# Two experts of 64 tokens in one gathered slot, multiplied in the two column halves of TensorE

## The chip, the cores and the metric

One Trainium2 chip, one core of it in use. The metric is device time in microseconds (us) of one launch, from the runs' own timer; the profile is one execution of the same program taken by the hardware profiler. TensorE appears as PE (matmuls) and PEld (weight loads), VectorE as DVE, ScalarE as ACT, GpSimd as POOL, SyncE as SP.

## What is computed

A two-layer backbone over 256 latent and 256 context tokens of width 1024. Each layer has a mixer (layer 0: a short gated convolution and a chunked gating MLP; layer 1: a conformer convolution and differential attention) and then a PEER channel mixer. All is float32. The mixer is left out here; the part that the change touches is this:

```python
def peer(h, wq, subkeys, u_tab, v_tab):
    t = h.reshape(-1, D_MODEL)
    q = (t @ wq).reshape(-1, PEER_HEADS, 2, PEER_QDIM // 2)
    s = jnp.einsum('thpd,hpkd->thpk', q, subkeys)
    sv, si = lax.top_k(s, PEER_TOPK)
    ...                      # 16 x 16 sums of both halves' scores, the best 16 of them
    idx = i1 * PEER_KEYS + i2
    g = jax.nn.softmax(cv, axis=-1)
    act = jax.nn.gelu(jnp.einsum('td,thkd->thk', tb, u_tab[ib]))
    return jnp.einsum('thk,thkd->td', gb * act, v_tab[ib])
```

Eight heads choose 16 of 16384 experts each, so every token reads 128 experts, and an expert is a row of `u_tab` and a row of `v_tab`, 1024 numbers each. The mixer is run three times: stage 0 (layer 0, latent tokens), stage 1 (layer 0, context tokens), stage 2 (layer 1, latent tokens).

## The kernel before, in words

Tokens lie on the 128 partitions; 256 tokens are two tiles. `u_tab` and `v_tab` are stored side by side, so an expert is one row of 8 KB in device memory. A **slot** is one expert for each of the 128 tokens of a tile: a gather of 128 rows, one per partition, into one of the eight places of the ring `uv`. There are 128 slots for a tile, 256 for a stage and 768 in all. For slot s:

- POOL (`gathers`, line 1050) waits until the place is free (`uv_used`) and issues the indirect transfer. The row numbers come from `idx`, a column per slot.
- DVE (`dot`, line 1593) waits for the landing and multiplies the u half with the tokens' rows `h2`, summing along the row: one number for each token.
- ACT (`weigh`, lines 1221, 1223, 1225) takes gelu of it, multiplies by the softmax weight `gw` and scales the identity with the result: `diag`, a 128 x 128 diagonal matrix.
- PE (`add_values`, line 983) multiplies `diag` with the v half, twice 512 columns, and sums in two banks of PSUM, `acc`, over the 128 slots of a tile. The last of the two matmuls raises `uv_used`.
- After the last slot of a tile DVE (`close`) multiplies `acc` by the gate and adds it to the token rows.

Everything else (projections, convolution, attention, queries, scores, the searches `find` that make `idx` and `gw`, conditioning) is cut into steps. `schedule` writes one list, `program`, in which slots, steps and values alternate: at slot s stands ("slot", s), then the takes that empty PSUM banks, then ("values", s - 2), as LAG is 2, then the steps whose place has come. Each engine walks this one list in its order (`walk`), doing its own part of every entry. So PE's order is values of one slot, some steps, values of the next, and PE does nothing at a "slot" entry, ACT and DVE nothing at "values".

`turn_back` (PE line 938, then ACT) makes the rows `h2` of a tile out of the transposed `hT`: eight transposes of 128 x 128 and two copies out of PSUM, once for each stage and tile, six in all. The first lies before slot 0, the first of stage 2 in the gap between slot 511 and slot 512; the others lie among slots. In front of slot 0 the places of the ring hold weights, and the first gathers wait for the products that read them (line 704 and line 768). `ada_pair` (line 704) multiplies conditioning weights in quarters of the array: for each k it issues quarters 0 and 1 out of one weight block and then quarters 2 and 3 out of the next block.

A search has six parts; the last (lines 1560 to 1576) writes the index of 16 experts (line 1564) and their weights (line 1569), one instruction each for a tile. Weights of the projections are loaded by SP through the same transfer engines.

## Time and profile before

| what | value |
|---|---|
| median of 3 runs | 2360.29 us (2359.01 to 2362.58) |
| span of the profiled execution | 2360.1 us |
| PE busy | 2079.7 us (88%), of which line 983 1447.1 us in 3072 records |
| DVE busy | 1609.6 us (68%), of which line 1593 935.1 us |
| ACT busy | 953.4 us (40%) |
| POOL busy | 1019.5 us (43%) |
| transfers | 939.43 MB, mean 398 GB/s |
| the chain that ended last | PE 36%, transfers 33%, DVE 13%, issue 7%, POOL 6%, ACT 5% |

Slots are gathered from 176 us on and from 1664 us on; before the one lies the first mixer, in between (1590 to 1664 us) the gap in which stage 1 ends and attention starts. A table of stretches shows, for each stretch, how long each engine was busy in it, the mean granted clock of PE and what was transferred. A line with "x12" stands for twelve records in a row.

### The profile page before, as it was taken

To read this page: it belongs to the slowest core of one execution; us is meant where nothing else is said; L and a number is where in the kernel's file an instruction comes from. 1 tells how busy PE (TensorE), PEld (TensorE's weight loads), DVE (VectorE), ACT (ScalarE), POOL (GpSimd) and SP (SyncE) were. 2 spreads that over 40 slices of the span, in tenths; PEclk is the share of its full clock that TensorE was granted. 3 is DMA by queue.
4 is the path that set the end of the run, shared out by engine and by line. 5 is a ranking of instruction groups with operands and counts; after the bars stand their busy time and mean duration, and the time that the engine had idled before them with its cause. 6 is when DMAs were issued, how large, how long until landed. Compare 5 with 4: busy or idle time off the path is not lost.

```text
span 2360.1 us, 24134 instructions
## 1 busy us (share of the span) xinstructions
PE 2079.7 (88%) x6896; PEld 1123.8 (48%) x6896; DVE 1609.6 (68%) x3952; ACT 953.4 (40%) x2791; POOL 1019.5 (43%) x868
## 2 busy tenths in 40 slices
PE   8998998899998988988898998798899988777787
PEld 7775554455564434544454544346455533222222
DVE  3855668967766568788866677855765887666454
ACT  2014434543334444444454333534543444444333
POOL 0004444344334444444444454530333555566774
PEclk9999999999999999999999999999999999999999
DMA  9979999999999999999999999996799999999997
GB/s 400 375 291 382 395 399 421 407 421 421 421 420 421 415 421 404 421 421 417 391 421 421 421 421 421 416 370 254 284 365 379 415 421 421 422 421 421 422 421 318
DMA packets 132595, 939.43 MB, mean 398 GB/s; under 512 B 14720, under 2 KB 17920, under 8 KB 18944
## 3 DMA queue, kind: packets, MB, share of 16 engines
q0 software_dynamic: 110592, 805.36, 82.8%
q1 hardware_dynamic: 21888, 132.68, 13.8%
q8 instruction: 55, 0.90, 0.2%
q14 instruction: 60, 0.49, 0.1%
HBM read 936.93 MB, written 1.05 MB: 397 GB/s over the span
## 4 chain that ended last, share of the span: by engine, by line
PE 36%; DMA 33%; DVE 13%; issue 7%; POOL 6%; ACT 5%; POOLq 0%; SPq 0%; DVEq 0%; ACTq 0%
DMA uv<-uv_dram,stage_idx 31%; PE psum L983 19%; PE psum L786 9%; DVE uv L1593 6%; POOL uv L1050 5%; PE psum L768 4%; PE psum L926 1%; DMA uv<-in_dram 1%; ACT diag L1225 1%; DMA uv<-ada_dram 1%; ACT wv L1223 1%; DVE h L1282 1%; PE psum L704 1%; PE psum L957 1%; ACT gel L1221 1%
## 5 line engine op out<-in xcount | busy, mean ns | idle before, releaser
L983 PE MATMUL psum<-uv,diag 128*128 128x512 f32 x3072 | 1447.1, 611 | 227.8 <-ACT diag L1225 217.6
L1050 POOL DMA_INDIRECT uv<-uv_dram,stage_idx x768 | 985.9, 1284 | 1052.3 <-PE psum L983 829.5
L1593 DVE CUSTOM_DVE_ANT_0 uv<-uv,h 128x1024 f32<-128x1024 f32 x768 | 935.1, 1226 | 554.6 <-DMA uv<-uv_dram,stage_idx 545.2
L983 PEld LDWEIGHTS psum<-uv,diag 128*128 128x128 f32 x3072 | 562.1, 192 | 1006.5 <-issue 505.3
L1221 ACT ACTIVATE gel<-dots 128x1 f32<-128x1 f32 x768 | 155.3, 202 | 1060.6 <-DVE dots L1593 1059.7
L1225 ACT ACTIVATE diag<-const,wv 128x128 f32<-128x128 f32 x768 | 308.3, 401 | 25.0
L786 PE MATMUL psum<-hT,wring 128*128 128x256 f32 (+1 forms) x1312 | 273.0, 361 | 0.7 <-ACT hT L1091 0.7
L786 PEld LDWEIGHTS psum<-hT,wring 128*128 128x128 f32 x1312 | 233.1, 190 | 60.2 <-issue 33.0
L1223 ACT ACTIVATE wv<-gel,gw 128x1 f32<-128x1 f32 x768 | 226.3, 295 | 25.0
L1038 POOL COPY stage_idx<-idx 128x8 uint32 (+1 forms) x96 | 33.4, 348 | 265.4 <-DVE idx L1564 264.7
L1073 ACT ACTIVATE work<-psum 128x256 f32<-128x256 f32 (+2 forms) x123 | 47.7, 389 | 128.5 <-PE psum L786 102.1
L768 PE MATMUL psum<-wring,hT 128*128 128x256 f32 x320 | 72.7, 382 | 0.7 <-ACT hT L1091 0.7
L768 PEld LDWEIGHTS psum<-wring,hT 128*128 128x128 f32 x320 | 61.6, 193 | 17.3 <-issue 8.8
L1221 ACT ACT_TABLE_LOAD x50 | 64.2, 1283 | 0.9
L1593 DVE DVE_READ_ACCUMULATOR2_ANT dots<- 128x1 f32 x768 | 62.8, 82 | 0.0
L786 PE MATMUL psum<-hT,uv 128*128 128x256 f32 (+1 forms) x224 | 52.4, 395 | 5.4 <-DVE sp_t L1364 2.8
L1532 DVE MAX8 work<-work 128x8 f32<-128x128 f32 x80 | 17.9, 279 | 50.8 <-ACT work L1073 50.7
L1401 DVE SCALAR_TENSOR_TENSOR work<-work,const 128x256 f32<-128x256 f32 x120 | 50.1, 478 | 0.0
L786 PEld LDWEIGHTS psum<-hT,uv 128*128 128x128 f32 x224 | 43.6, 208 | 13.3 <-issue 5.7
L1192 ACT ACT_TABLE_LOAD x32 | 41.1, 1283 | 0.6
L957 PEld LDWEIGHTS psum<-keys,work 128*128 128x128 f32 x192 | 26.6, 197 | 18.2 <-issue 11.6
L1282 DVE CUSTOM_DVE_ANT_0 h<-uv,h 128x1024 f32<-128x1024 f32 x28 | 33.2, 1221 | 3.0 <-issue 2.3
(224 smaller groups left out, 1289.8 us busy)
## 6 DMA issues: line engine op xcount, KB each, us to landing
uv<-ada_dram SPq DMA_DIRECT2D x30, 1024.0 KB, 15.8
wring<-in_dram SPq DMA_DIRECT2D x25, 1024.0 KB, 9.5
wring<-wq_dram SPq DMA_DIRECT2D x24, 1024.0 KB, 11.2
uv<-uv_dram,stage_idx POOLq DMA_INDIRECT x768, 14.2
uv<-in_dram SPq DMA_DIRECT2D x9, 1024.0 KB, 13.5
uv<-ada_t_dram SPq DMA_DIRECT2D x7, 1024.0 KB, 22.7
wring<-ada_dram SPq DMA_DIRECT2D x6, 1024.0 KB, 11.2
wring<-ada_t_dram SPq DMA_DIRECT2D x5, 1024.0 KB, 20.7
```

What stands on the lines that cost most here:

```text
L768: last = mm(bank[:, 0:BLK], src[:, k, :], w[:, k, :], start=(k == 0), stop=(k == KC - 1))
L786: last = mm(bank[:, 0:len(tiles) * P], w[:, k, i * P:(i + 1) * P], hT[:, k, tokens], start=(k == 0), stop=(k == KC - 1))
L957: last = mm(bank[:, o:o + P], qh[:, h % 2, q, t * P:(t + 1) * P], keys[:, h % 2, q * PK:(q + 1) * PK], start=True, stop=True)
L983: last = mm(acc[:, b, :], diag[:, s % RING, :], uv[:, s % RING, D + 512 * b:D + 512 * (b + 1)], start=(c == 0), stop=(c == NSEL - 1))
L1050: nc.gpsimd.indirect_dma_start(out=uv[:, s, :], out_offset=None, in_=tables[stage // 2], in_offset=bass.IndirectOffsetOnAxis(ap=stage_idx[ ...
L1073: mine.emptied(f(dst, src, func, **kw))
L1221: f(gel[:, r:r + 1], dots[:, r:r + 1], ACT.Gelu_apprx_tanh).then_inc(gelu_ready, 1)
L1223: f(wv[:, r:r + 1], gel[:, r:r + 1], ACT.Copy, scale=gw[:, (T // TT) % 2, T % TT, c:c + 1]).then_inc(wv_ready, 1)
L1225: f(diag[:, r, :], C("ident"), ACT.Copy, scale=wv[:, r:r + 1]).then_inc(diag_ready, 1)
L1282: v.tensor_tensor_reduce(out=row_tmp[:, j, :], in0=w, in1=c_rows[:, j, :], scale=1.0, scalar=0.0, op0=ALU.mult, op1=ALU.add, accum_out=ada ...
L1401: ops = [v.scalar_tensor_tensor(out=ccT[:, j, :], in0=cpT[:, j, k:k + TOK], scalar=w[:, j, k:k + 1], in1=ccT[:, j, :], op0=ALU.mult, op1=A ...
L1593: v.tensor_tensor_reduce(out=uv[:, r, 0:D], in0=uv[:, r, 0:D], in1=h2[:, row_of[stage], t, :], scale=1.0, scalar=0.0, op0=ALU.mult, op1=AL ...
```

## The change

A slot no longer holds one expert for each of 128 tokens but two experts for each of 64: partitions 0 to 63 hold the first expert, partitions 64 to 127 the second one, of the same 64 tokens. Slot 2m has tokens 0 to 63 of the tile, slot 2m + 1 tokens 64 to 127, both the experts 2m and 2m + 1. The number of slots, of rows and of bytes is the same. With it go:

- `diag` has 64 columns (two diagonals on top of one another, from `pair_ident`, which DVE makes once at the start), and the matmul writes 64 partitions of `acc`: the upper or the lower half, so the left or the right columns of the array. Contraction over 128 partitions sums both experts.
- the values of an even slot are put in the list right before those of the odd one, both at the place where the odd one's stood.
- `h2` has two forms for each tile, one for each half of tokens, with the 64 rows on both halves of the partitions; `turn_back` makes them by products with the identity, and ACT copies four banks.
- index and weight are written by four instructions instead of one, each for 64 partitions and every second column.
- the space that gathers' descriptors get in SBUF is set to 4096 bytes per partition.

```diff
+HALVES = 2
+HT = P // HALVES
+SCRATCH = 4096
@@ schedule
-            if v >= (0 if stage < 2 else first):
-                program.append(("values", v))
+            if v >= (0 if stage < 2 else first) and v % HALVES == HALVES - 1:
+                program += [("values", u) for u in range(v - HALVES + 1, v + 1)]
@@ build
-        h2 = sb("h2", [P, 2, TT, D])
+        h2 = sb("h2", [P, 2, TT, HALVES, D])
-        diag = sb("diag", [P, RING, P])
+        diag = sb("diag", [P, RING, HT])
+        pair_ident = sb("pair_ident", [P, HT])
+        ALL_HALVES = [(k, j) for k in range(HALVES) for j in range(HALVES)]
+        def rows_of(half):
+            return slice(half * HT, (half + 1) * HT)
@@ PE turn_back
-                for half in range(2):
-                    bank = to_act.open(pe)
-                    for i in range(4):
-                        last = turn(bank[:, i * P:(i + 1) * P], hT[:, half * 4 + i, t * P:(t + 1) * P], ident)
-                    to_act.fill(last)
+                for j in range(HALVES):
+                    half_tile = slice(t * P + j * HT, t * P + (j + 1) * HT)
+                    for half in range(2):
+                        bank = to_act.open(pe)
+                        for i in range(4):
+                            for k in range(HALVES):
+                                last = mm(bank[rows_of(k), i * P:(i + 1) * P], hT[:, half * 4 + i, half_tile], ident, start=True, stop=True)
+                        to_act.fill(last)
@@ PE add_values
+                j = c % HALVES
                 for b in range(2):
-                    last = mm(acc[:, b, :], diag[:, s % RING, :], uv[:, s % RING, D + 512 * b:D + 512 * (b + 1)],
-                              start=(c == 0), stop=(c == NSEL - 1))
+                    last = mm(acc[j * HT:(j + 1) * HT, b, :], diag[:, s % RING, :], uv[:, s % RING, D + 512 * b:D + 512 * (b + 1)],
+                              start=(c < HALVES), stop=(c >= NSEL - HALVES))
@@ ACT turn_back, weigh
-                for half in range(2):
-                    empty(h2[:, row_of[stage], t, half * 512:(half + 1) * 512], 512)
+                for j in range(HALVES):
+                    for half in range(2):
+                        empty(h2[:, row_of[stage], t, j, half * 512:(half + 1) * 512], 512)
-                f(diag[:, r, :], C("ident"), ACT.Copy, scale=wv[:, r:r + 1]).then_inc(diag_ready, 1)
+                f(diag[:, r, :], pair_ident[:, :], ACT.Copy, scale=wv[:, r:r + 1]).then_inc(diag_ready, 1)
+            act.wait_ge(pairs_set, 1)
@@ DVE find, last part
-                        v.scalar_tensor_tensor(out=idx[:, stage % 2, t, slots[i]], in0=w.side_no[:, a + i, :], scalar=float(PK),
-                                               in1=w.side_no[:, n_t + a + i, :], op0=ALU.mult, op1=ALU.add).then_inc(idx_ready[t], 1)
+                        for k, j in ALL_HALVES:
+                            done = v.scalar_tensor_tensor(out=pairs[rows_of(k), :, j], in0=first[rows_of(j), :, k], scalar=float(PK),
+                                                          in1=second[rows_of(j), :, k], op0=ALU.mult, op1=ALU.add)
+                        done.then_inc(idx_ready[t], 1)
...
+                        for half, j in ALL_HALVES:
+                            done = v.tensor_scalar(pairs[rows_of(half), :, j], terms[rows_of(j), :, half],
+                                                   w.e_stat[rows_of(j), 1, a + i:a + i + 1], None, ALU.mult)
@@ DVE dot, start
-                v.tensor_tensor_reduce(out=uv[:, r, 0:D], in0=uv[:, r, 0:D], in1=h2[:, row_of[stage], t, :], scale=1.0, scalar=0.0,
+                v.tensor_tensor_reduce(out=uv[:, r, 0:D], in0=uv[:, r, 0:D], in1=h2[:, row_of[stage], t, s % HALVES, :], scale=1.0, scalar=0.0,
+            v.tensor_tensor(pair_ident[:, :], C("ident")[:, 0:HT], C("ident")[:, HT:P], ALU.add).then_inc(pairs_set, 1)
@@ kernel
-    nc = bacc.Bacc("TRN2", target_bir_lowering=False, num_devices=1)
+    nc = bacc.Bacc("TRN2", target_bir_lowering=False, num_devices=1, dynamic_dma_scratch_size=SCRATCH)
```

## Rows read from the trace of the kernel before

**Rows 1.** The page's slices of 59 us: transfer rate.
```profile
GB/s 400 375 291 382 395 399 421 407 421 421 421 420 421 415 421 404 421 421 417 391 421 421 421 421 421 416 370 254 284 365 379 415 421 421 422 421 421 422 421 318
```
**Rows 2.** Stretches: length, busy us (instructions) PE, PEld, DVE, ACT, POOL; clock, share, GB/s.
```profile
200.00:330.00 130.00, 120.62 (x441) 73.89 (x440) 75.36 (x203) 53.51 (x161) 54.32 (x49) 0.99 0.99 397
...
470.00:920.00 450.00, 416.62 (x1257) 231.06 (x1256) 297.15 (x701) 177.88 (x540) 208.57 (x185) 1.00 1.01 420
...
1120.00:1180.00 60.00, 53.47 (x153) 28.50 (x153) 50.81 (x149) 27.89 (x81) 25.20 (x26) 0.97 0.97 392
...
1540.00:1590.00 50.00, 48.80 (x113) 20.96 (x112) 28.72 (x46) 19.49 (x62) 15.82 (x15) 1.00 0.92 361
...
1700.00:1760.00 60.00, 54.38 (x193) 30.40 (x192) 39.98 (x105) 28.32 (x76) 19.92 (x21) 1.00 0.92 361
...
1800.00:1840.00 40.00, 39.53 (x144) 25.04 (x143) 25.11 (x84) 17.82 (x53) 14.52 (x14) 1.00 0.92 353
1840.00:2330.00 490.00, 395.88 (x845) 149.35 (x843) 323.70 (x769) 196.60 (x612) 305.58 (x222) 0.98 1.01 421
```
**Rows 3.** The chain that ended last, in order of time: start, duration, what.
```profile
1575.89 10.42 DMA uv<-uv_dram,stage_idx
...
1797.00 3.47 PE psum L786 x16
...
1815.04 5.15 PE psum L983 x12
```
**Rows 4.** The same stretches, line 983 alone: length, PE busy, PEld busy, clock, share, GB/s.
```profile
200.00:330.00 130.00, 77.48 (x169) 30.91 (x168) 0.99 0.99 397
...
470.00:920.00 450.00, 300.53 (x657) 121.07 (x656) 1.00 1.01 420
...
1540.00:1590.00 50.00, 36.91 (x83) 15.71 (x84) 1.00 0.92 361
...
1700.00:1760.00 60.00, 33.73 (x74) 12.91 (x72) 1.00 0.92 361
...
1800.00:1840.00 40.00, 23.29 (x53) 10.07 (x54) 1.00 0.92 353
```
**Rows 5.** Waits from 200 to 330 us: us in total, times, longest.
```profile
POOL uv L1050 <- PE psum L983: 65.3, 25, 5.4
```
**Rows 6.** Timeline of PE from 1133 us: start, duration, records, [idle before].
```profile
1138.84 3.49 PE L983 MATMUL psum<-uv,diag 128*128 128x512 f32 x4 [1.88 <-ACT diag L1225]
```
**Rows 7.** Timeline of PE from 173.4 us: quarters of the array, line 704.
```profile
173.52 0.41 PE L704 MATMUL psum<-wring,silu_c 128*32 128x256 f32 x2
173.54 0.41 PE L704 MATMUL psum<-uv,silu_c 128*32 128x256 f32 x2
173.74 0.41 PE L704 MATMUL psum<-wring,silu_c 128*32 128x256 f32 x2
```
**Rows 8.** Line 1050, the gathers: time from issue to landing.
```profile
DMA to landing us min/median/max: 5.4/14.2/18.6
```
**Rows 9.** Timeline of all engines around the first turn_back (line 938) and first gather.
```profile
160.50 3.82 PE L786 MATMUL psum<-hT,wring 128*128 128x128 f32 x32
...
165.23 1.04 PE L938 MATMUL psum<-const,hT 128*128 128x128 f32 x8
...
165.87 1.08 ACT L1073 ACTIVATE h<-psum 128x512 f32<-128x512 f32 x2
...
176.04 1.09 POOL L1050 DMA_INDIRECT uv<-uv_dram,stage_idx  x1 [0.97 <-PE psum L704]
```
**Rows 10.** Groups of instructions by form: count, busy us, mean ns, idle before.
```profile
L1225 ACT ACTIVATE diag<-const,wv 128x128 f32<-128x128 f32 x768 | 308.3, 401 | 25.0
...
L1569 DVE TENSOR_SCALAR gw<-work 128x16 f32<-128x16 f32 x44 | 8.9, 239 | 1.0
...
L1564 DVE SCALAR_TENSOR_TENSOR idx<-work 128x16 uint32<-128x16 f32 x44 | 6.4, 172 | 1.0
```
**Rows 11.** The page's transfer queues: the gathers' queue.
```profile
q0 software_dynamic: 110592, 805.36, 82.8%
```

More of the change, by code:

```diff
@@ L506, in build @@
         row_of = (0, 1, 1)
-        c_rows = h2[:, 0, :, :]
-        row_tmp = h2[:, 1, :, :]
+        c_rows = h2[:, 0, 0, :, :]
+        row_tmp = h2[:, 1, 0, :, :]
         kept_sc = vx[:, :, :].rearrange("p a (b c) -> p (a b) c", c=2 * PK).rearrange("p h (q k) -> p h q k", q=2)
@@ L1563, in find @@
                     for i, t in enumerate(tiles):
-                        v.scalar_tensor_tensor(out=idx[:, stage % 2, t, slots[i]], in0=w.side_no[:, a + i, :], scalar=float(PK),
-                                               in1=w.side_no[:, n_t + a + i, :], op0=ALU.mult, op1=ALU.add).then_inc(idx_ready[t], 1)
+                        pairs = idx[:, stage % 2, t, slots[i]].rearrange("p (m j) -> p m j", j=HALVES)
+                        first, second = (w.side_no[:, q * n_t + a + i, :].rearrange("p (m k) -> p m k", k=HALVES) for q in range(2))
+                        for k, j in ALL_HALVES:
+                            done = v.scalar_tensor_tensor(out=pairs[rows_of(k), :, j], in0=first[rows_of(j), :, k], scalar=float(PK),
+                                                          in1=second[rows_of(j), :, k], op0=ALU.mult, op1=ALU.add)
+                        done.then_inc(idx_ready[t], 1)
                     dve.wait_ge(exp_ready, n["exp"])
@@ L1568, in find @@
                     link(v.reciprocal(w.e_stat[:, 1, a:b], w.e_stat[:, 0, a:b]))
-                    weights = [v.tensor_scalar(gw[:, stage % 2, t, slots[i]], w.e16[:, a + i, :], w.e_stat[:, 1, a + i:a + i + 1], None,
-                                               ALU.mult) for i, t in enumerate(tiles)]
-                    link(*weights[:-1])
+                    for i, t in enumerate(tiles):
+                        pairs = gw[:, stage % 2, t, slots[i]].rearrange("p (m j) -> p m j", j=HALVES)
+                        terms = w.e16[:, a + i, :].rearrange("p (m k) -> p m k", k=HALVES)
+                        for half, j in ALL_HALVES:
+                            done = v.tensor_scalar(pairs[rows_of(half), :, j], terms[rows_of(j), :, half],
+                                                   w.e_stat[rows_of(j), 1, a + i:a + i + 1], None, ALU.mult)
                     if kept(stage, h, tiles):
-                        link(weights[-1])
+                        link(done)
                     else:
-                        weights[-1].then_inc(sc_used, 1)
+                        done.then_inc(sc_used, 1)
                         dve.wait_ge(sc_used, k)
@@ L1601, in close @@
                 dve.wait_ge(*taken["gate", stage, 1])
-                tmp = h2[:, row_of[stage], t, :]
+                tmp = h2[:, row_of[stage], t, 0, :]
                 v.tensor_tensor(tmp, acc.rearrange("p a b -> p (a b)"), gate_peer[:, :], ALU.mult).then_inc(acc_free, 1)
```

8 lines of the change are left out of this document (4 added, 4 removed).

## The prediction

> **What bounds the kernel now.** I read the slices of the page first, then a table of chosen stretches, then the same table for line 983 alone, and only then single instructions. The slices show one number again and again: 421 GB/s [rows 1]. No slice is above 422, and in the table the stretches at 420 or 421 GB/s have a DMA share of 1.01 [rows 2]: the transfer engines are full there. A gathered slot moves 128 rows of 8 KB, 1.05 MB, which at 421 GB/s takes 2.49 us. 768 such slots are 1913 us of the 2360. In those stretches (470 to 920 us, 1840 to 2330 us, and most of what lies between 330 and 1540) nothing that is done on TensorE can make the kernel faster, however busy PE is.
>
> So what the change can be worth lies where the rate is below 421 while gathers run. For a stretch of length L at rate r the loss is L x (1 - r/421): 130 us at 397 lose 7.4 us; 60 at 392 (from 1120) lose 4.1; 50 at 361 (from 1540) lose 7.1; 60 at 361 (from 1700) lose 8.6; 40 at 353 (from 1800) lose 6.5 [rows 2]. From the stretch at 1540 I take off the end: the last gather of that stage is issued at 1575.89 and lands 10.42 us later [rows 3], so from 1586.3 to 1590 there is nothing to transfer; 3.4 us are left to win. Together 30.0 us, 25.9 without the stretch from 1120.
>
> Is PE what holds these stretches? In the four it is busy for 120.62 of 130, 48.80 of 50, 54.38 of 60 and 39.53 of 40 us [rows 2], and line 983, the values, is 77.48, 36.91, 33.73 and 23.29 us of that [rows 4]. GpSimd, which issues the gathers, waits there for line 983: 65.3 us in the first stretch [rows 5]. The stretch from 1120 is another case: there a slot's four records took 3.49 us where others take 1.72, after 1.88 us of idle [rows 6], and the granted clock of the stretch is 0.97 [rows 2]; that is the lower of the two levels for a few us.
>
> **The change, part by part.** *The values.* A slot has two float32 matmuls and each is two records, so four records of 512 columns; twelve in a row take 5.15 us [rows 3], 0.43 each, 1.72 per slot, 3.43 per pair. After it each matmul has the same 128 rows and 512 columns but writes 64 columns of the array, and the two slots of a pair write different halves. If the halves run side by side, a pair whose two diagonals are ready costs 1.72. Does hardware do that? The conditioning products (line 704) already use quarters. For each k the code issues quarters 0 and 1 from one weight block, then 2 and 3 from the other, each as two records, so four records of the first block stand in the program before four of the second. The trace shows two of wring and two of uv start within 0.04 us, and the next two of wring 0.22 us after the first [rows 7], just a record's time at 256 columns (3.47 us for 16, [rows 3]). So four quarters run at once, and the second record of a quarter that is still busy doesn't hold back the first of another. I take the full overlap: 0.86 us less per slot where PE is behind. Where PE is not behind, the odd slot's diagonal comes 2.5 us after the even one's, the halves run one after the other, and nothing changes.
>
> The Trainium skill speaks against this ("TensorE: Matmul & The Clock Gate", Part 3, The mechanism): matmuls start and end strictly in program order, none passes another. By that rule the second slot's first record could only overlap the first slot's fourth, and a pair would take seven records' time, 3.0 us. The alternation in the trace disagrees with it for quarters; for halves no row here decides.
>
> Half of line 983's time in the four stretches is 38.7, 18.5, 16.9 and 11.6 us, each more than the loss there (7.4, 3.4, 8.6, 6.5). PE would stop being last, and the transfers would be. Against it: going from full width to half width and back may cost something at each step that stands between pairs. Bounds: nothing, or one idle record of 0.43 us [rows 3]. In the first stretch the other work is 43.1 us, some 12 steps of 3.47, so 24 turns and at most 10 us of the 38.7 freed: no decision hangs on it, and I take nothing. As PE isn't full in two of the four (93% and 91%), part of the loss must be waits of other engines in turn. I take two thirds of 25.9: 17.3 us gained; ends 8 and 30.
>
> *The order.* Even slots' values move behind one more set of PE steps, up to 3.47 us later [rows 3], and the next gather into that slot with them; the odd ones lose the 1.72 of the even slot in front. The ring has eight slots, 19.9 us per turn at 2.49. From issue to landing it takes 14.2 us, and 5.4 at the least [rows 8]: 8.8 us of the flight are queueing, so a release later by 3.5 leaves the transfers full. I cost it at nothing; its price without that cover is among the rivals.
>
> *turn_back.* Eight records at 1.04 us [rows 9] become 32 matmuls, 64 records: no longer transposes but products with the identity, each chunk for both row halves. Records of 128 columns run at 3.82 us for 32 [rows 9], 0.119 each; side by side 32 of them in time, 3.8 us, so +2.8 per call; one after the other 7.6, +6.6. Four of the six calls lie inside streams of slots, beside transfers that are last. Two do not: before slot 0, where the first gather waits for line 704, which stands behind turn_back on PE [rows 9], and in the gap before slot 512, where PE's later steps (attention, queries) stand behind it and slots 512 on wait for PE. I count both: 5.6 us. ACT empties four banks in place of two, 1.08 us more [rows 9], beside PE's longer run.
>
> *The lists.* Index and weight of a head and tile become four instructions each: 3 x 0.172 + 3 x 0.239 = 1.2 us more DVE [rows 10], of which the three index ones, 0.5 us, are ahead of the gather. At slot 0 the wait for line 704 covers them; in the gap they are bare: 0.5 us. Elsewhere DVE delays a dot by 1.2 to 2.5 us per search, inside the 8.8 us of queueing.
>
> *Small ones.* The diagonal is 64 columns instead of 128, on ACT 401 ns now [rows 10]: at most half, 0.2 us, saved per slot, and no gain where transfers are last. One addition at the start, pair_ident, for which ACT waits: one DVE instruction, nothing to some 0.3 us, and I take nothing. The descriptor space given to gathers falls to 4096: 110592 packets for 768 gathers [rows 11] are 144 each, 9 per engine, 72 for all eight slots. The Trainium skill ("DMA: Bandwidth & Descriptors", Terms) gives a descriptor as 16 bytes, by which 4096 bytes would be 256 of them; no run here shows it. I take nothing.
>
> Sum: 2360.3 - 17.3 + 5.6 + 0.5 = 2349. The profiled execution's span is 2360.1 and the median 2360.29, so no shift is needed.
>
> **The rivals.** *Freed PE time doesn't become transfer time*: the stretches are a ring of waits (a search on DVE waits for scores on ACT, these for PE's queries, these for a bank), and only the lower end, 8 us, comes back: 2360.3 - 8 + 6.1 = 2358, no change that can be told. For it: PE's 7 to 9% idle there. Against: nearly 100% in the other two.
>
> *The halves don't overlap, in program order*: a pair takes 3.0 of 3.43 us, so 0.21 per slot, an eighth of line 983's time: 9.7 us of PE freed in the first stretch and 3 to 5 in the others; perhaps 8 us of transfer time, minus the 6.1: also 2358. So the change not doing what it says ends there too, not on the slow side.
>
> *The ring starves (slower)*: place: each search of a head, 24 in all, when a step of 3.47 us stands before an even slot's values and the longer search delays the odd dot. Dots are late by 1.2 to 2.5 us, the release by 3.47, and it decides once both together with the waits already there pass 8.8 us. If every search then costs the transfers 1 us, it is +24, with the gains of the forecast halved (8.6) and the costs 6.1: 2360 + 24 - 9 + 6 = 2381; at half of that 2369.
>
> *The clock*: PE is idle more, and with half the columns at work. At the lower level a four-record slot takes 3.49 us [rows 6]. From 470 to 920 the values would need 150 us as pairs and the rest 116 [rows 2, 4]; at the lower level all the time 532 of 450 us, far slower, but PE fits in as long as the lower level holds for under about 69% of the stretch (266 x 1.69 = 450). I see no row that speaks for so much.
>
> **How the numbers follow.** Forecast, gain beyond 0.2% (4.7 us, about what a measurement can tell): 0.53, own range 2333 (30 us back, one turn_back bare: 2360 - 30 + 3) to 2355. No change, by the first two rivals: 0.27 (0.18 and 0.09). Slower: 0.20, the ring 0.14, at 2369 to 2381, the clock 0.04 and the descriptor space 0.02, both far out. The range goes from 2333 to 2371: it leaves out a few hundredths below and half of the slow cases or a little more.
>
> **What would show it.** Right: in the changed trace records of line 983 of a pair start within hundredths of a us of each other in the stretches after slot 0 and after slot 512, those stretches read near 421 GB/s, and GpSimd's wait for line 983 there shrinks; the stretches at 421 stay as they are; the first gather comes about 3 us later. Wrong: pairs of 3 us or more where both diagonals are ready, new slices below 415 in the middle of a stage, a granted clock well under 0.97, or full overlap with the same rates as before.

## The result and the profile after

The kernel became slower, by a little: 2367.74 us median (2363.22 to 2372.6, 12 runs) beside 2362.14 (2358.87 to 2364.91, 12 runs) of the kernel before, a ratio of 1.0028 with a 95% interval of 1.0019 to 1.0036. The forecast was 2349, faster. The profiled execution spans 2368.4 us. In this section and the next a difference in microseconds is the ratio of a run less one, times 2362: the changed kernel stands at +6.6.

In the profile after, `add_values` is line 999 (983 before), the gathers 1066 (1050), the dots 1618 (1593), the diagonal 1242 (1225), `turn_back` 953 on PE and 1089 on ACT (938, 1073), index and weight 1585 and 1595 (1564, 1569), the projections 798 (786).

The page of after, busy time and slices; they answer to the table of before and [rows 1]:

```profile
PE 1935.7 (82%) x7232; PEld 909.9 (38%) x7232; DVE 1675.3 (71%) x4241; ACT 919.8 (39%) x2803; POOL 928.2 (39%) x868
...
GB/s 402 371 289 359 386 420 421 388 408 421 421 420 421 402 420 420 420 420 409 401 421 420 421 421 419 416 373 260 259 367 392 421 408 421 421 421 421 421 421 320
```

PE lost 144 us of work and the kernel still lost time. The slices say where: 359 and 386 from 177 us on were 382 and 395 before, 388 and 408 from 413 us on were 407 and 421, 259 from about 1655 us on was 284, and there are new ones at 402, 409 and 408 where 415 to 421 stood.

The stretches of after; columns as in [rows 2], and the row of before for 430 to 470 us, which the prediction did not read, in the second fence:

```profile
200.00:330.00 130.00, 108.73 (x495) 62.63 (x493) 77.22 (x205) 52.70 (x163) 53.13 (x50) 0.93 0.96 389
430.00:470.00 40.00, 33.05 (x116) 15.99 (x117) 38.12 (x119) 19.61 (x61) 16.36 (x15) 0.91 0.94 371
1540.00:1590.00 50.00, 45.35 (x123) 14.05 (x122) 29.82 (x48) 17.57 (x62) 20.29 (x19) 1.00 0.97 401
1700.00:1760.00 60.00, 50.43 (x244) 27.08 (x241) 41.29 (x106) 29.16 (x79) 23.25 (x22) 0.93 0.83 329
1800.00:1840.00 40.00, 37.56 (x161) 22.61 (x160) 28.34 (x81) 15.66 (x54) 15.94 (x16) 0.96 0.98 401
1840.00:2330.00 490.00, 362.91 (x847) 104.57 (x846) 344.14 (x859) 187.50 (x610) 239.01 (x220) 0.96 1.01 420
```

```profile
430.00:470.00 40.00, 36.43 (x111) 20.70 (x110) 35.32 (x106) 19.70 (x60) 15.39 (x14) 0.96 1.00 401
```

Two of the stretches that were to be won are won in part (353 became 401 from 1800 us, 361 became 401 from 1540), two are worse though PE is less busy in them (397 became 389, 361 became 329), and a new one is lost at 430 us, where DVE is busy for 38.12 of 40 us.

A stretch is fixed in time while the slots in it shift, so these rates are a first look. The gathers, counted in GpSimd's timelines, are surer. Beside before, the 32nd gather is issued 4.9 us later in the changed kernel, the 112th 8.8, the 512th 3.0, the 513th (the first after the gap) 6.6 and the last 8.4. So time is lost in the first 112 slots and after slot 511, and none on balance between them. This is one execution of each kernel.

PE, then GpSimd, of after from 263 us, in the first stretch (start, duration, records, [idle before]):

```profile
267.30 7.77 PE L798 MATMUL psum<-hT,wring 128*128 128x256 f32 x32
...
276.18 3.70 PE L999 MATMUL psum<-uv,diag 128*64 128x512 f32 x16
```

```profile
268.17 0.94 POOL L1066 DMA_INDIRECT uv<-uv_dram,stage_idx  x1 [8.46 <-PE psum L999]
...
278.93 1.06 POOL L1066 DMA_INDIRECT uv<-uv_dram,stage_idx  x1 [8.38 <-PE psum L999]
280.30 1.06 POOL L1066 DMA_INDIRECT uv<-uv_dram,stage_idx  x1 [0.31 <-issue]
```

The same engines in the trace of before; its two gathers belong to the slots of the last two above, the 33rd and 34th:

```profile
268.73 3.62 PE L786 MATMUL psum<-hT,wring 128*128 128x256 f32 x16
...
273.37 7.03 PE L983 MATMUL psum<-uv,diag 128*128 128x512 f32 x16
```

```profile
269.71 0.96 POOL L1050 DMA_INDIRECT uv<-uv_dram,stage_idx  x1 [4.04 <-PE psum L983]
276.06 1.19 POOL L1050 DMA_INDIRECT uv<-uv_dram,stage_idx  x1 [5.39 <-PE psum L983]
```

Sixteen records, four slots, take 3.70 us where sixteen full ones took 7.03: the halves do run side by side. But before them stand two projections in a row (x32, 7.77 us), and GpSimd waits 8.4 us, twice, for a place in the ring. Each time it then gets two places at once, so two slots waited 8.69 us here and 9.43 before: later and in bursts, but not longer. Its total wait for the values is no measure either. It grew over the kernel from 829.5 us to 913.9, while its own issues took 97 us less, and it is 944.5 in halves_alone below, which is faster than before.

### The profile page after: what moved, and what is told of

It reads as the page before. It is cut to its first block, busy times and chain, and to the rows that moved or that the text cites. A ratio compares the mean times of both kernels' runs of the same rounds, so it can differ in the third digit from the quotient of the medians.

```text
span 2368.4 us, 25105 instructions
## 1 busy us (share of the span) xinstructions
PE 1935.7 (82%) x7232; PEld 909.9 (38%) x7232; DVE 1675.3 (71%) x4241; ACT 919.8 (39%) x2803; POOL 928.2 (39%) x868
## 4 chain that ended last, share of the span: by engine, by line
DMA 41%; PE 26%; DVE 21%; issue 6%; ACT 5%; POOL 1%; POOLq 0%; SPq 0%; DVEq 0%; ACTq 0%
DMA uv<-uv_dram,stage_idx 39%; PE psum L999 11%; DVE uv L1618 9%; PE psum L798 7%; PE psum L780 3%; DVE gw L1595 1%; ACT diag L1242 1%; DMA uv<-in_dram 1%; PE psum L953 1%; POOL uv L1066 1%; ACT wv L1240 1%; DMA uv<-ada_dram 1%; DVE idx L1585 1%; DVE work L1579 1%; PE psum L716 1%
## 5 line engine op out<-in xcount | busy, mean ns | idle before, releaser
L999 PE MATMUL psum<-uv,diag 128*64 128x512 f32 x3072 | 1231.7, 640 | 350.6 <-ACT diag L1242 341.0
L1066 POOL DMA_INDIRECT uv<-uv_dram,stage_idx x768 | 888.8, 1157 | 1145.7 <-PE psum L999 913.9
L999 PEld LDWEIGHTS psum<-uv,diag 128*64 128x64 f32 x3072 | 333.6, 143 | 1147.7 <-ACT diag L1242 686.4
L798 PE MATMUL psum<-hT,wring 128*128 128x256 f32 (+1 forms) x1312 | 281.8, 369 | 0.7 <-ACT hT L1107 0.7
L1242 ACT ACTIVATE diag<-pair_ident,wv 128x64 f32<-128x64 f32 x768 | 267.1, 348 | 25.0
L1054 POOL COPY stage_idx<-idx 128x8 uint32 (+1 forms) x96 | 39.2, 409 | 270.6 <-DVE idx L1585 270.0
L972 PE MATMUL psum<-keys,work 128*128 128x128 f32 x192 | 33.6, 317 | 18.4 <-ACT work L1089 18.4
L1595 DVE TENSOR_SCALAR gw<-work 64x8 f32<-64x8 f32 x176 | 43.3, 246 | 3.2
L972 PEld LDWEIGHTS psum<-keys,work 128*128 128x128 f32 x192 | 27.0, 213 | 42.7 <-ACT work L1089 22.9
```

Of the source, the lines that this page charges most:

```text
L798: last = mm(bank[:, 0:len(tiles) * P], w[:, k, i * P:(i + 1) * P], hT[:, k, tokens], start=(k == 0), stop=(k == KC - 1))
L972: last = mm(bank[:, o:o + P], qh[:, h % 2, q, t * P:(t + 1) * P], keys[:, h % 2, q * PK:(q + 1) * PK], start=True, stop=True)
L999: last = mm(acc[j * HT:(j + 1) * HT, b, :], diag[:, s % RING, :], uv[:, s % RING, D + 512 * b:D + 512 * (b + 1)], start=(c < HALVES), stop ...
L1066: nc.gpsimd.indirect_dma_start(out=uv[:, s, :], out_offset=None, in_=tables[stage // 2], in_offset=bass.IndirectOffsetOnAxis(ap=stage_idx[ ...
L1242: f(diag[:, r, :], pair_ident[:, :], ACT.Copy, scale=wv[:, r:r + 1]).then_inc(diag_ready, 1)
L1595: done = v.tensor_scalar(pairs[rows_of(half), :, j], terms[rows_of(j), :, half], w.e_stat[rows_of(j), 1, a + i:a + i + 1], None, ALU.mult)
```

## The experiments

All numbers together, as ratio to the kernel before, run beside each on the same chip (95% interval), and difference:

| kernel | ratio | us |
|---|---|---|
| the changed kernel | 1.0028 (1.0019 to 1.0036) | +6.6 |
| before_pairs | 1.0020 (1.0009 to 1.0031) | +4.7 |
| before_narrow | 1.0036 (1.0024 to 1.0048) | +8.5 |
| before_space | 0.9997 (0.9986 to 1.0008) | -0.7 |
| one_half | 1.0125 (1.0109 to 1.0140) | +29.5 |
| own_place | 1.0083 (1.0069 to 1.0097) | +19.6 |
| pair_early | 1.0017 (1.0007 to 1.0026) | +4.0 |
| halves_alone | 0.9966 (0.9954 to 0.9979) | -8.0 |
| halves_early | 0.9959 (0.9946 to 0.9972) | -9.7 |
| old_lists | 0.9987 (0.9977 to 0.9996) | -3.1 |
| old_turn | 0.9986 (0.9973 to 0.9999) | -3.3 |
| turn_copies | 1.0010 (1.0001 to 1.0019) | +2.4 |
| lean | 1.0004 (0.9995 to 1.0012) | +0.9 |
| lean_both | 1.0002 (0.9990 to 1.0014) | +0.5 |
| lean_copies | 1.0002 (0.9992 to 1.0012) | +0.5 |

An interval is about 2 to 3 us to either side, so differences of two rows are good to 3 or 4 us. Several results lie outside the range that the theory they were made for had given, or between two ranges: one_half a little above its range, own_place and old_turn outside theirs, and before_pairs, before_narrow, halves_early, lean, lean_both, turn_copies and lean_copies between two.

**Overlap and order.** The first theory: the halves overlap, and the ring starves because values stand later in the list. Four kernels take order and overlap apart.

*one_half*, the changed kernel, all slots but the second of a tile in one half:

```diff
-                j = c % HALVES
+                j = 1 if c == 1 else 0
-                              start=(c < HALVES), stop=(c >= NSEL - HALVES))
+                              start=(c < HALVES), stop=(c == 1 or c == NSEL - 1))
```

> The changed kernel, but the values of all slots of a tile except the second go to the same half of the array's columns, so the two slots of a pair can't run side by side (the sums of the two token halves are mixed up by that). All waits, instructions and their order are those of the changed kernel. Theory A, with overlap worth the PE time that the records show: 6 to 20 us slower than the changed kernel, 2374 to 2388 us. If the overlap is worth nothing, since transfers or searches are last wherever PE is behind: 2366 to 2370 us. Rival C (clock): the granted clock rises, since PE is busy longer, towards 0.98.

Measured 2389.1 us. Overlap is worth 22.9 us beside the changed kernel. The run also shows that something costs much more than the forecast's 6.1 us: without overlap the change is 29.5 us slower than before.

*own_place*, the changed kernel with values at their own places:

```diff
-            if v >= (0 if stage < 2 else first) and v % HALVES == HALVES - 1:
-                program += [("values", u) for u in range(v - HALVES + 1, v + 1)]
+            if v >= (0 if stage < 2 else first):
+                program.append(("values", v))
```

> The changed kernel with one part undone: the values of every slot stand at their own place in the list again (slot s - 2), halves, lists, turn_back and descriptor space as changed. Theory A (the order costs the time: two sets of PE steps stand in a row before an even slot's values, its ring place and that of its neighbour come back late and together, and the transfers run dry): the new dips go, 2356 to 2362 us, and the stretches from 430 to 470 and 1700 to 1760 us are back near 401 and 361 GB/s. Rival B (the fixed additions cost it: turn_back, lists, descriptor space): stays at 2365 to 2369 us. Rival C (the lower clock costs it, because PE works with half the columns): stays at 2365 to 2369 us with a mean granted clock near 0.95.

2379.16 us. Slots then meet only where no step stands between them, and 13 us are lost beside the changed kernel; a part of that can be the changes of width priced below, of which single slots make more than pairs. So the pairs in the list are needed, and order is not the main cost.

*before_pairs*, the kernel before with pairs in the list and nothing else:

```diff
-            if v >= (0 if stage < 2 else first):
-                program.append(("values", v))
+            if v >= (0 if stage < 2 else first) and v % HALVES == HALVES - 1:
+                program += [("values", u) for u in range(v - HALVES + 1, v + 1)]
```

> The kernel before with one part of the change alone: the values of an even slot stand right before those of the odd one, at the odd one's place; 128 columns, old lists, old turn_back, old descriptor space. Nothing can overlap. Theory A: slower than before by 8 to 25 us (2370 to 2387), with dips where steps are dense (200 to 330 and 1700 to 1840 us). Rival B and C: no difference beyond 0.2%, 2358 to 2366 us.

2367.1 us, +4.7: moving values behind one more step has a price by itself, though its lower bound is only 2 us.

*pair_early*, the changed kernel with the pair where the even slot stood:

```diff
-            v = s - LAG
+            v = s - LAG + 1
```

> The changed kernel with the pair moved one place forward: both slots' values stand where the even slot's stood before the change (the odd one's now one slot behind its dot instead of two). The halves can still overlap. Theory A: both places come back earlier, 2346 to 2358 us, faster than before the change. Rival B: 2363 to 2369 us, as the additions stay. Rival C: 2363 to 2369 us. If PE's wait for the odd slot's diagonal now holds up the steps behind it (queries, so searches), it is slower than the changed kernel: 2370 to 2385 us.

2364.65 us, 2.6 better than the changed kernel, which is within the noise of such a difference, and still slower than before. The order may be a part of the loss; it isn't the loss.

**Width and additions.** own_place and one_half could be slow for two reasons: matmuls of half width, or the additional work in lists and turn_back.

*before_narrow*, the kernel before with half-width values that never overlap:

```diff
-        diag = sb("diag", [P, RING, P])
+        diag = sb("diag", [P, RING, 64])
...
-                    last = mm(acc[:, b, :], diag[:, s % RING, :], uv[:, s % RING, D + 512 * b:D + 512 * (b + 1)],
-                              start=(c == 0), stop=(c == NSEL - 1))
+                    last = mm(acc[64 * (c == 1):64 * (c == 1) + 64, b, :], diag[:, s % RING, :], uv[:, s % RING, D + 512 * b:D + 512 * (b + 1)],
+                              start=(c < 2), stop=(c == 1 or c == NSEL - 1))
...
-                f(diag[:, r, :], C("ident"), ACT.Copy, scale=wv[:, r:r + 1]).then_inc(diag_ready, 1)
+                f(diag[:, r, :], C("ident")[:, 0:64], ACT.Copy, scale=wv[:, r:r + 1]).then_inc(diag_ready, 1)
```

> The kernel before with only the width changed: the diagonal has 64 columns and every slot (but the second of a tile) writes the same 64 partitions of acc, each at its own place in the list; nothing overlaps, lists, turn_back and order are as before (half of the output is left out). Theory of the width: each change between full and half width costs about 0.2 us, some 0.4 for each round of one slot and one step, so where PE is last (200 to 330 us and 1660 to 1840 us, some 100 rounds) it loses 20 us or more: 2372 to 2390 beside 2361, nearly what own_place (2379) and one_half (2389) showed. Theory of the additions (lists and turn_back make these two slow, width is free as the prediction said): 2358 to 2363.

2369.06 us, +8.5: less than the theory of the width gave, but not nothing. The same piece of PE's work shows the price. First the kernel before, then before_narrow (start, duration, records):

```profile
1814.87 5.32 PE L983 MATMUL psum<-uv,diag 128*128 128x512 f32 x12
1820.03 3.62 PE L786 MATMUL psum<-hT,wring 128*128 128x256 f32 x16
1823.48 5.31 PE L983 MATMUL psum<-uv,diag 128*128 128x512 f32 x12
1828.63 1.05 PE L738 MATMUL psum<-gdiag,ones 128*128 128x128 f32 x8
1829.52 5.32 PE L983 MATMUL psum<-uv,diag 128*128 128x512 f32 x12
```

```profile
1820.03 5.36 PE L983 MATMUL psum<-uv,diag 128*64 128x512 f32 x12
1825.33 3.72 PE L786 MATMUL psum<-hT,wring 128*128 128x256 f32 x16
1828.98 5.36 PE L983 MATMUL psum<-uv,diag 128*64 128x512 f32 x12
1834.27 1.16 PE L738 MATMUL psum<-gdiag,ones 128*128 128x128 f32 x8
1835.36 5.36 PE L983 MATMUL psum<-uv,diag 128*64 128x512 f32 x12
```

From the first start to the last it is 14.65 us and 15.33 for the same work with four changes of width: 0.17 us for each change (0.14 from half to full, 0.20 from full to half). No half-width work stood next to full-width work in the trace of before, but the quarters of [rows 7] did. The record that follows their last step, which starts at 175.03 us:

```profile
175.39 0.38 PE L719 MATMUL psum<-const,ada_rows 128*128 128x4 f32 x2
```

Eight steps, 173.52 to 175.03, are 0.216 us from one to the next, but the full-width record starts 0.36 us after the last of them: 0.14 us more. So a price could be read before the change.

The mean granted clock of its trace is 0.990, beside 0.981 before, so half the columns at work do not by themselves lower the clock. The stretches of before_narrow, for [rows 2]; PE is as busy as before and the rates are lower:

```profile
200.00:330.00 130.00, 119.61 (x426) 60.65 (x425) 74.40 (x202) 51.19 (x160) 47.18 (x46) 1.00 0.97 384
...
1700.00:1760.00 60.00, 55.10 (x180) 24.50 (x179) 38.00 (x99) 27.02 (x74) 20.68 (x20) 1.00 0.88 336
1800.00:1840.00 40.00, 39.53 (x138) 20.96 (x137) 20.99 (x61) 12.66 (x44) 13.05 (x13) 1.00 0.86 323
```

*halves_alone*, halves, pairs and the diagonal of 64 columns put into the kernel before, whose lists and turn_back stay:

```diff
-            if v >= (0 if stage < 2 else first):
-                program.append(("values", v))
+            if v >= (0 if stage < 2 else first) and v % 2 == 1:
+                program += [("values", u) for u in (v - 1, v)]
...
-                    last = mm(acc[:, b, :], diag[:, s % RING, :], uv[:, s % RING, D + 512 * b:D + 512 * (b + 1)],
-                              start=(c == 0), stop=(c == NSEL - 1))
+                    last = mm(acc[64 * (c % 2):64 * (c % 2) + 64, b, :], diag[:, s % RING, :], uv[:, s % RING, D + 512 * b:D + 512 * (b + 1)],
+                              start=(c < 2), stop=(c >= NSEL - 2))
...
```

> The kernel before with values in two halves, 64-column diagonals and the order of pairs, but with the lists and turn_back of before (so it multiplies other rows than it should, its output isn't the reference's). It is the change without its additions on DVE and in turn_back. If lists and turn_back ate the gain: 2345 to 2356, the forecast. If order and width did: 2361 to 2367, within a few us of the changed kernel's 2368.

2354.68 us, faster than before by 8.0 us. This is the mechanism of the forecast at work. Its stretches, and PE from 286 us:

```profile
200.00:330.00 130.00, 109.43 (x454) 61.91 (x455) 80.93 (x216) 52.60 (x165) 53.55 (x52) 0.95 1.00 409
...
1700.00:1760.00 60.00, 51.40 (x221) 27.00 (x219) 39.50 (x99) 27.27 (x83) 20.16 (x22) 0.94 0.95 382
1800.00:1840.00 40.00, 34.51 (x131) 16.37 (x130) 31.16 (x89) 15.73 (x48) 22.99 (x20) 0.96 0.99 403
```

```profile
286.46 1.94 PE L983 MATMUL psum<-uv,diag 128*64 128x512 f32 x8
288.36 1.16 PE L957 MATMUL psum<-keys,work 128*128 128x128 f32 x8
```

A pair takes 1.90 us from its start to that of the next step, where two slots of full width take 3.43. Rates rise to 409, 382 and 403: PE isn't last there any more, but the transfers aren't full either. Counted as above, the same five gathers are issued 5.4, 5.0, 9.0, 5.0 and 10.4 us earlier than before. Beside the changed kernel that is 10.3, 13.8, 12.0, 11.6 and 18.8 us: what halves_alone leaves out costs time in the first 112 slots and after the gap, and next to nothing between them, where transfers are last.

*halves_early* is halves_alone with the one line of pair_early (`v = s - LAG + 1`):

> halves_alone with the pair at the even slot's place: the odd slot's values wait for a diagonal that is just being made, but no release of a place is late. halves_alone gave 2355. If a late release is what is left of the order's cost: 2349 to 2352. If PE's wait for the odd diagonal costs as much: 2355 to 2358.

2354.18 us: no difference that can be told from halves_alone. With the additions gone, the later place of the pair costs nothing that can be measured (1.7 us, good to 3 or 4).

**Which addition.** *old_lists* is the changed kernel with index and weight as before (the rest of the edit puts `link` back):

```diff
-                        for k, j in ALL_HALVES:
-                            done = v.scalar_tensor_tensor(out=pairs[rows_of(k), :, j], ...
+                        v.scalar_tensor_tensor(out=idx[:, stage % 2, t, slots[i]], in0=w.side_no[:, a + i, :], scalar=float(PK),
+                                               in1=w.side_no[:, n_t + a + i, :], op0=ALU.mult, op1=ALU.add).then_inc(idx_ready[t], 1)
...
-                        for half, j in ALL_HALVES:
-                            done = v.tensor_scalar(pairs[rows_of(half), :, j], ...
+                    weights = [v.tensor_scalar(gw[:, stage % 2, t, slots[i]], w.e16[:, a + i, :], w.e_stat[:, 1, a + i:a + i + 1], None,
+                                               ALU.mult) for i, t in enumerate(tiles)]
```

> The changed kernel with index and weight written by one instruction for each tile as before (experts then stand at the wrong tokens: the output isn't the reference's). Theory that the longer searches cost transfers where DVE is nearly full (38.1 of 40 us from 430 to 470 us): 2359 to 2364, and the rate from 430 to 470 us back from 371 to about 400 GB/s. Theory that they are covered: 2366 to 2369 as the changed kernel.

*old_turn* is the changed kernel with turn_back as before:

```diff
-                for j in range(HALVES):
-                    half_tile = slice(t * P + j * HT, t * P + (j + 1) * HT)
...
+                        last = turn(bank[:, i * P:(i + 1) * P], hT[:, half * 4 + i, t * P:(t + 1) * P], ident)
...
-                        empty(h2[:, row_of[stage], t, j, half * 512:(half + 1) * 512], 512)
+                    empty(h2[:, row_of[stage], t, 0, half * 512:(half + 1) * 512], 512)
...
-in1=h2[:, row_of[stage], t, s % HALVES, :]
+in1=h2[:, row_of[stage], t, 0, :]
```

> The changed kernel with turn_back as before: eight transposes, two copies, one form of the rows (dots use the wrong half's order, so the output isn't the reference's). The prediction's term says 5.6 us less for two bare calls: 2362. The first gather of the changed kernel was only 0.5 us later, so I now expect less: 2364 to 2367.

2360.26 and 2359.27 us: each gives back 10 us, both together (halves_alone) 14.6. So with the other one gone each costs 5. That the two prices don't add is not clear of noise: the 5 us between 19.6 and 14.6 come out of four rows, each good to 2 or 3. Stretches of old_lists, then of old_turn:

```profile
430.00:470.00 40.00, 34.53 (x130) 17.57 (x129) 34.78 (x103) 19.37 (x60) 19.62 (x18) 1.00 1.00 405
```

```profile
200.00:330.00 130.00, 109.98 (x453) 60.31 (x452) 82.98 (x228) 53.16 (x168) 50.11 (x52) 0.95 1.00 406
430.00:470.00 40.00, 35.83 (x123) 18.51 (x124) 33.78 (x110) 17.82 (x56) 16.33 (x16) 0.87 0.89 357
1700.00:1760.00 60.00, 52.74 (x218) 27.29 (x214) 44.18 (x119) 28.03 (x79) 23.74 (x23) 0.94 0.95 382
```

Without the longer lists the dip at 430 us is gone (405, DVE 34.78 of 40); without the longer turn_back it stays (357), and the stretches at 200 and 1700 us are back.

*before_space*, the kernel before with another descriptor space:

```diff
-    nc = bacc.Bacc("TRN2", target_bir_lowering=False, num_devices=1)
+    nc = bacc.Bacc("TRN2", target_bir_lowering=False, num_devices=1, dynamic_dma_scratch_size=4096)
```

> The kernel before with the descriptor space of gathers set to 4096 bytes and nothing else. Costed at nothing: 2360 to 2364, ratio 1.000 within 0.001. If the space were short, gathers would be issued later: 2370 or more.

2362.16 us: no effect, as the prediction had it.

**A better version.** *lean* is pair_early, with the weights written by DVE as before and spread by ACT:

```diff
+                if c % TOPK == 0:
+                    pairs = gx[:, g, :].rearrange("p (m j) -> p m j", j=HALVES)
+                    terms = gw[:, (T // TT) % 2, T % TT, c:c + TOPK].rearrange("p (m k) -> p m k", k=HALVES)
+                    for k, j in ALL_HALVES:
+                        f(pairs[rows_of(k), :, j], terms[rows_of(j), :, k], ACT.Copy).then_inc(crossed, 1)
```

> The changed kernel with two edits: the pair stands at the even slot's place (one slot earlier), and DVE writes the weights in their own order by one instruction for each tile; ACT spreads them by four small copies when it weighs the first of 16 slots. The index keeps its four instructions. pair_early alone gave 2365 and the whole of the lists is worth 7.5 us (old_lists 2360). If the lists cost by DVE's time, the weights are 0.71 of the 1.2 us for each tile: about 4.5 us, 2359 to 2362. If it is the index, which stands ahead of the gather, that costs: 2364 to 2366.

2363.86 us, 5.7 better than the changed kernel and no faster than before. *lean_both* writes in addition the index of both tiles by the same four instructions:

```diff
+                    for k, j in ALL_HALVES:
+                        done = v.scalar_tensor_tensor(out=pairs[rows_of(k), :, :, j], in0=first[rows_of(j), :, :, k], scalar=float(PK),
+                                                      in1=second[rows_of(j), :, :, k], op0=ALU.mult, op1=ALU.add)
+                    done.then_inc(idx_ready[tiles[0]], 1)
```

> The kernel lean with the four index instructions of a search written for both tiles at once where it has both, so four for a search and not eight. DVE then does nearly what it did before the change. With the lists' 7.5 us all back and the pair at the even slot's place: 2356 to 2360, a little faster than the kernel before (2361 to 2363). If the cost is in something else of the lists than their number: 2362 to 2366.

2361.72 us, the same as lean and as before. The 6 us are back, but no more. *turn_copies* moves turn_back's work to ACT, and *lean_copies* does that in lean_both:

```diff
+                for half in range(2):
+                    bank = mine.full_bank(act)
+                    for k, j in ALL_HALVES:
+                        last = f(h2[rows_of(k), row_of[stage], t, j, half * 512:(half + 1) * 512], bank[rows_of(j), :], ACT.Copy)
+                    mine.emptied(last)
```

> The changed kernel with turn_back's work moved from PE to ACT: eight transposes as before the change, and ACT makes both forms of the rows by eight copies of 64 partitions (each 0.6 us now) out of the two banks, 4.8 us of ACT where the changed kernel has 2.4 and the kernel before 1.2. If turn_back costs by PE's time (3.7 in place of 1.0 us): most of what old_turn gave back, 2359 to 2362. If it costs by ACT's copies, for which dots and banks wait: 2368 to 2373.

> The kernel lean_both with the same turn_back by copies. If turn_back costs by PE's time: 2353 to 2358, faster than the kernel before. If by ACT's copies: 2362 to 2367.

2363.33 us, 4 better than the changed kernel, and 2360.84, the same as lean_both. Moving the work to ACT gives back 4 of the 10 us that old_turn did, a difference beyond the noise by little. From the trace of turn_copies the row that may tell why, copies of 4.83 us in all, after 1.97 us of transposes on PE:

```profile
220.59 4.83 ACT L1184 ACTIVATE h<-psum 64x512 f32<-64x512 f32 x8
```

In the code the dots of that tile wait for these copies; what that wait cost was not traced. Of the versions that do all of the kernel's work, none was faster than the kernel before.

## Why the prediction was wrong, step by step

**The bound: right, but for one stretch.** Where transfers were full they stayed so (420 GB/s from 1840 us), and halves_alone gained in stretches that the prediction named. One that loses wasn't on its list: 430 to 470 us, 401 GB/s before, hidden in a slice that read 407 [rows 1], with DVE busy for 35.32 of 40 us. I asked of each stretch whether PE was what held it, and never where DVE was nearly full. The sign that GpSimd's wait for line 983 would shrink was no good: from 200 to 330 us it is 65.3 us before, 64.7 after and 67.2 in halves_alone.

**The overlap: right, its sign and its size.** Eight records take 1.90 us to the start of the next step; overlap is worth 22.9 us (one_half to the changed kernel). The program-order rule that I quoted from the Trainium skill ("TensorE: Matmul & The Clock Gate", Part 3, The mechanism) would give a pair 3.0 us; the trace disagrees with it for halves too, as the quarters of [rows 7] had said. *The halves don't overlap* is refuted.

**What the overlap brings in transfers: 17.3 us said, 8.0 measured.** This is the first step that failed. I took two thirds of the 25.9 us that the stretches lose, since PE would stop being last there. It did: in halves_alone PE is busy for 109.43 of 130, 51.40 of 60 and 34.51 of 40 us. But the rates are 409, 382 and 403, not 421, so about half of those three losses is still there (an estimate by the forecast's own formula: 11.0 of 22.5 us). Of the stretch before the gap, where I had counted 3.4 us, little lasts: the last gather of stage 1 is issued 9.0 us earlier than before, the first of stage 2 only 5.0. The next two paragraphs name two prices in it that I had put at nothing. How the missing 9.3 us divide between them, the waits of other engines in turn and the lower clock (0.95 in the first stretch, 0.99 before) no run tells.

**The width: a term costed at nothing that measured 8.5 us by itself.** The prediction bounded it at 0.43 us a turn, said that no decision hangs on it, and took the lower end. It is 0.17 us a change, and PE pays it twice for each pair that stands between steps, in just those stretches where PE is last. The 8.5 us are before_narrow's, where PE is nearly full and every slot stands alone; with pairs and a PE that has time left the price can only be guessed to be less. The Trainium skill ("TensorEngine Tiling (Array Packing)", Key Properties) says that a change of tiling mode drains TensorE; the trace agrees that a change costs time, 0.17 us here. Where a bound times a count (24 turns, 10 us) is as large as the gain itself, its lower end is no forecast.

**The order: about 5 us alone, 2 to 3 with the halves and there within the noise, costed at nothing.** The cover of 8.8 us was worked out from the median flight of all gathers [rows 8]. Where PE is behind, gathers don't queue as long: in the trace of before those issued from 200 to 330 us have

```profile
DMA to landing us min/median/max: 5.6/9.6/13.8
```

and from 1700 and from 1800 us the medians are 8.6 and 8.7. So the cover there was 3 to 4 us, and a release later by 3.5 could use it up.

**The lists: 0.5 us said, 5 to 10 measured.** The count was right: DVE's busy time grew by 65.7 us, and a group of the page shows how ([rows 10] for before):

```profile
L1595 DVE TENSOR_SCALAR gw<-work 64x8 f32<-64x8 f32 x176 | 43.3, 246 | 3.2
```

An instruction for a quarter of the numbers takes as long as one for all. At the end of the search at 430 us index and weights of both tiles stand between two dots, in before and then in after:

```profile
436.76 0.26 DVE L1564 SCALAR_TENSOR_TENSOR idx<-work 128x16 uint32<-128x16 f32 x2
...
437.35 0.37 DVE L1569 TENSOR_SCALAR gw<-work 128x16 f32<-128x16 f32 x2
```

```profile
439.50 1.41 DVE L1585 SCALAR_TENSOR_TENSOR idx<-work 64x8 uint32<-64x8 f32 x8
...
441.36 2.15 DVE L1595 TENSOR_SCALAR gw<-work 64x8 f32<-64x8 f32 x8
```

The next dot starts 6.5 us after the one in front of it (437.05 to 443.54), before 3.6 (434.31 to 437.86): 2.9 us later, on an engine that has no idle time there. The prediction had 1.2 to 2.5, and the cover was again the 8.8 us; the gathers issued from 430 to 470 us before have a median flight of 8.9 and a least one of 6.2.

**turn_back: 5.6 us said, 5 to 10 measured.** The duration was right, the places weren't, so where the sum came near it was luck. In the gap, by the rows of before and then of after:

```profile
1655.83 1.04 PE L938 MATMUL psum<-const,hT 128*128 128x128 f32 x8
1656.80 1.14 PE L862 MATMUL psum<-h 64*128 64x256 f32 x8
```

```profile
217.04 5.51 PE L953 MATMUL psum<-const,hT 128*64 128x128 f32 x64 [1.81 <-ACT hT L1107]
...
1661.97 3.71 PE L953 MATMUL psum<-const,hT 128*64 128x128 f32 x64
1665.62 1.14 PE L874 MATMUL psum<-h 64*128 64x256 f32 x8
...
1728.77 5.69 PE L953 MATMUL psum<-const,hT 128*64 128x128 f32 x64 [2.17 <-ACT hT L1107]
```

0.97 us became 3.65 there, the +2.7 of the sum. Before slot 0 little of it arrived: the first gather is issued 0.5 us later. But the calls at 217 and 1729 us, which I had put among streams where transfers are last, lie in two of my own four stretches where PE is last, and took 5.5 and 5.7 us: PE had been idle for 1.8 and 2.2 us ahead of them, and the granted clock over them was 0.66 and 0.63, a part of the time at the lower of the two levels (1.00 over the call in the gap). The short calls of old_turn at these two places met the lower level too and took 1.97 us each. The rows of after, then of old_turn:

```profile
217.04:222.50 5.46, 5.46 (x66) 5.46 (x68) 3.17 (x7) 2.64 (x6) 0.00 (x0) 0.66 1.02 422
1728.80:1734.30 5.50, 5.50 (x66) 5.50 (x67) 5.05 (x10) 2.64 (x6) 0.00 (x0) 0.63 0.80 329
```

```profile
214.94 1.97 PE L950 MATMUL psum<-const,hT 128*128 128x128 f32 x8 [1.61 <-ACT hT L1104]
...
1720.13 1.97 PE L950 MATMUL psum<-const,hT 128*128 128x128 f32 x8 [1.69 <-ACT hT L1104]
```

By these rows (an estimate) the long calls cost PE 3.5, 3.7 and, in the gap, 2.7 us: 9.9 in all, as much as old_turn gave back.

**The sum.** Predicted: -17.3 for the values with width and order at nothing, and +6.1 for the additions. Measured: -8.0 for the values with width and order (halves_alone), and +14.6 for the additions (halves_alone to the changed kernel): +6.6. The forecast was missed by two like parts, 9.3 us in the values and 8.5 in the additions. The rival *freed PE time doesn't become transfer time* had the values' net right (8 us), and what it named is what halves_alone shows: PE with time left and transfers that are not full; its sum missed by the additions alone. Of *the ring starves* the longer searches did cost time, at a lower price than it named; that late values made them dearer was not seen (2.6 us with the additions, 1.7 without). The descriptor space did nothing. In the rival *the clock* the 69% are a share of the work, not of the stretch: at half speed for 82% of the 450 us PE still does its 266.

**What stays open.** How the values' 8.0 us come about, as said above. The clock's own share: its mean fell from 0.981 to 0.952, halves_alone was faster than before at 0.970, and no run changed the clock alone. Whether the two additions, 5 us each alone and 14.6 together, make each other dearer. That GpSimd could spread the index was not tried.

## What to carry to other kernels

Packing two products into the column halves of the array saves PE 1.5 us of 3.4 for a pair, but it pays only if what makes the operands fit costs less; here index, weights and rows in paired order cost 14.6 us, nearly twice the net gain of 8.0. Price an addition at the stretch in which it stands, not at the kernel's average: a median that holds over all gathers says nothing of the stretch where PE or DVE is last. Taking the first engine off the path brings back what the next wait allows, which here was 8.0 of 25.9 us. And where the price of a step has bounds of nothing and as much as the gain, take neither end: such a step is the forecast's main risk.

## What the runs showed of the hardware

Half-width records run beside those of the other half out of program order: eight of a pair took 1.94 us in halves_alone, where twelve that all write one half took 5.36 in before_narrow. A change between full and half width costs 0.17 us on PE. A DVE instruction on 64 x 8 numbers took 246 ns, one on 128 x 16 took 239 [rows 10]. A diagonal of 64 columns took ACT 348 ns instead of 401, and an issue of a gather on GpSimd took 1171 ns instead of 1284 in before_narrow, where nothing of GpSimd's work was touched; the cause was not looked for. The rows of before and before_narrow:

```profile
L1050 POOL DMA_INDIRECT uv<-uv_dram,stage_idx x768 | 985.9, 1284 | 1052.3 <-PE psum L983 829.5 <-issue 158.7 <-POOL stage_idx L1038 48.8
```

```profile
L1050 POOL DMA_INDIRECT uv<-uv_dram,stage_idx x768 | 899.4, 1171 | 1145.4 <-PE psum L983 970.4 <-issue 125.7 <-POOL stage_idx L1038 34.5
```
